# Hybrid decoder layer with 64 experts on one core: the experts' second weights requested by GpSimd on a second queue, the forget gate in column tiles, the last scatter in two halves

## The reference

```python
mod = (c_act @ ada_w[l] + ada_b[l]).reshape(B, N_MOD, D_MODEL)
h = rms_norm(x, mix_norm_g[l]) * (1.0 + scale_m) + shift_m
mix = mixer_sublayer(h, ...)           # pooling, spatial gating, convolution, attention with a forget gate
x = x + gate_m * mix
h = rms_norm(x, ffn_norm_g[l]) * (1.0 + scale_f) + shift_f
ffn = moe_ffn(h, ...)
x = x + gate_f * ffn
return rms_norm(x, final_norm_g)

# in the attention: four heads, a forget gate of four columns of w_in
log_f = jax.nn.log_sigmoid(f_logit.astype(jnp.float32))
cum = jnp.cumsum(log_f, axis=1)
logits = logits + c_blk[..., None] - cum_k[:, :, None, :]

# in the feed-forward part: 64 experts, 6 of them for each token, and one shared expert
a = jnp.einsum('td,edf->tef', tc, w1)
b = jnp.einsum('td,edf->tef', tc, w3)
hid = jax.nn.silu(a) * b * gc[:, :, None].astype(tc.dtype)
return jnp.einsum('tef,efd->td', hid, w2)
```

## Time and profile before

| | |
|---|---|
| time, median of 3 runs | 780.5 us (780.03 to 780.75) |
| profiled execution: time, span | 781.12 us, 779.3 us |
| mean granted TensorE clock | 0.989 |
| busy: PE, PEld, DVE, ACT, POOL | 730.0, 387.9, 326.3, 172.2, 8.7 us |
| moved by DMA | 271.33 MB, mean 348 GB/s |

### The profile page before, as it was taken

How to read it: one execution, slowest core, us unless ns; L and a number is a source line. 1 busy time by engine, 2 the same in 40 slices (tenths; PEclk the granted TensorE clock), 3 DMA queues, 4 the chain that set the end, 5 groups by cost and what they waited for, 6 DMA issues and landing times.

```text
span 779.3 us, 12407 instructions
## 1 busy us (share of the span) xinstructions
PE 730.0 (94%) x5000; PEld 387.9 (50%) x5000; DVE 326.3 (42%) x814; ACT 172.2 (22%) x344; POOL 8.7 (1%) x22
## 2 busy tenths in 40 slices
PE   4799999999999999999999999999999999899894
PEld 1388888888887444334333343333334333333232
DVE  1107675674446577333334233231333333323325
ACT  3213240200000241222222122121222222212213
POOL 0200001000000000000000000000000000000000
PEclk9799999999999999999999999999999999999998
DMA  9999535777869676999999999999999999999981
GB/s 339 378 349 365 190 108 189 237 260 259 264 221 385 262 274 240 392 422 421 421 417 420 419 420 421 421 421 408 409 420 422 420 419 422 421 421 420 421 353 55
DMA packets 73571, 271.33 MB, mean 348 GB/s; under 512 B 4440, under 2 KB 33248, under 8 KB 48688
## 3 DMA queue, kind: packets, MB, share of 16 engines
q1 hardware_dynamic: 71808, 264.26, 86.3%
q0 software_dynamic: 1408, 6.20, 2.1%
q10 hardware_dynamic: 304, 0.13, 0.1%
HBM read 269.51 MB, written 1.05 MB: 347 GB/s over the span
## 4 chain that ended last, share of the span: by engine, by line
PE 67%; DMA 21%; DVE 6%; SPq 3%; ACT 2%; issue 1%; DVEq 0%; ACTq 0%
PE bank L1118 65%; DMA ring<-exp_w_dram 19%; DMA ring<-ada_w_dram 2%; SPq L364 1%; DVE slot_gate L1054 1%; SPq L361 1%; PE bank L1438 1%; DVE reg L1058 1%; DVE reg L1049 1%; ACT reg L632 1%; DMA reg<-reg 1%; DVE h_hT L1109 0%; PE bank L1138 0%; DVE stats L1096 0%; DVE bank L1072 0%
## 5 line engine op out<-in xcount | busy, mean ns | idle before, releaser
L1118 PE MATMUL bank<-ring,h_hT 128*32 128x512 f32 (+2 forms) x2112 | 255.4, 586 | 14.3 <-DMA ring<-exp_w_dram 13.5
L1118 PEld LDWEIGHTS bank<-ring,h_hT 128*32 128x32 f32 (+1 forms) x2112 | 84.6, 113 | 170.8 <-issue 151.2
L1118 PE MATMUL bank<-h_hT,ring 128*128 128x256 f32 x704 | 158.4, 385 | 1.8 <-ACT h_hT L478 1.8
L1118 PEld LDWEIGHTS bank<-h_hT,ring 128*128 128x128 f32 x704 | 135.5, 193 | 21.4 <-ACT h_hT L478 2.0
L1118 PE MATMUL bank<-ring,const_misc 128*32 128x512 f32 x1008 | 116.5, 595 | 0.3
L1049 DVE TENSOR_TENSOR reg<-reg,bank 128x256 f32<-128x256 f32 x32 | 13.5, 421 | 180.7 <-ACT reg L632 180.7
L1072 DVE TENSOR_TENSOR bank<-bank,reg 128x512 f32<-128x512 f32 x64 | 44.5, 695 | 54.6 <-PE bank L1118 54.6
L1076 DVE TENSOR_TENSOR y_part<-bank,y_part 128x512 fp32r<-128x512 f32 x64 | 44.3, 692 | 42.4 <-ACT y_part L645 21.2
L1118 PEld LDWEIGHTS bank<-ring,const_misc 128*32 128x32 f32 x1008 | 30.2, 109 | 61.6 <-issue 57.3
L632 ACT ACTIVATE reg<-bank 128x256 f32<-128x256 f32 x32 | 12.3, 384 | 198.8 <-PE bank L1118 198.8
L1118 PE MATMUL bank<-take,h_part 128*128 128x256 f32 x288 | 50.6, 299 | 0.4 <-ACT h_hT L617 0.2
(11 more groups left out here) (231 smaller groups left out, 450.5 us busy)
## 6 DMA issues: line engine op xcount, KB each, us to landing
ring<-exp_w_dram SPq DMA_DIRECT2D x189, 1024.0 KB, 14.9
ring<-ada_w_dram SPq DMA_DIRECT2D x24, 1024.0 KB, 12.5
ring<-w_in_dram SPq DMA_DIRECT2D x24, 1024.0 KB, 12.3
ring<-w_branch_dram SPq DMA_DIRECT2D x4, 1024.0 KB, 12.9
ring<-w_out_dram SPq DMA_DIRECT2D x4, 1024.0 KB, 8.0
ring<-shared_w_dram SPq DMA_DIRECT2D x2, 1024.0 KB, 13.8
spare<-exp_w_dram SPq DMA_DIRECT2D x2, 1024.0 KB, 16.2
reg<-ada_bp_dram POOLq DMA_DIRECT2D x3, 512.0 KB, 8.3
```

The lines of the kernel that those rows point to most:

```text
L1118: return pe.matmul(o, lhsT, rhs, start=start, stop=stop, skip_group_check=True)
```

## The change

Three edits.

1. SP no longer requests second weights. GpSimd does, in a loop of its own that waits for `w2_used[r]` and goes by its own queue (the profile's q0, software; SP's is q1, hardware). For pairs 0 and 1 its requests stand before and after its request of `final_g`.
2. The forget gate's 8 matmuls write four groups of 32 partitions of bank 7 (the weights are padded from 4 to 32 columns), so that four can run side by side and the groups hold partial sums. ScalarE copies them (`f_tiles`), and one more matmul with a 0/1 matrix (`fold_f`) adds the groups, placed between the two halves of the key unit.
3. `y_split` becomes `y_low` and `y_high`: the gate matmul and the low half of a scatter wait for the low half alone, the high half of the scatter for the high one; the same after the last pair.

```diff
-MISC = {"wf": KD * HEADS, "sg_w": HEADS * P, ...}
+MISC = {"wf": KD * 32, "sg_w": HEADS * P, ...}
...
 @block.sync
-            def load_2(r, e, it):
-                sp.dma_start(ring[:, 6 * r + 4 + e, :],
-                             w2_src[bass.ds(it * (2 * RING_PAIRS) + (2 * r + e), 1)].rearrange("e p n -> (e p) n"))\
-                  .then_inc(w2_landed[r], 16)
...
             def load_step(use, it, spared=False):
                 for r in range(RING_PAIRS):
...
-                    sp.wait_ge(w2_used[r], use)
-                    for e in range(spared and r == SPARE_PAIR % 2, 2):
-                        load_2(r, e, it)
...
-                for e in range(2):
-                    sp.wait_ge(*used_up(LAST[6 * r + 4 + e]))
-                    load_2(r, e, 0)
...
 @block.gpsimd
+            def first_load_2(r):
+                for e in range(2):
+                    pool.wait_ge(*used_up(LAST[6 * r + 4 + e]))
+                    pool.dma_start(ring[:, 6 * r + 4 + e, :], w2_src[2 * r + e]).then_inc(w2_landed[r], 16)
+
+            first_load_2(0)
             pool.wait_ge(S["h2_done"], TB)
             pool.dma_start(final_g, a["final_norm_g"].rearrange("(o d) -> o d", o=1).partition_broadcast(P))\
                 .then_inc(S["final_in"], 16)
+            first_load_2(1)
+
+            def load_2(use, it, spared=False):
+
+                for r in range(RING_PAIRS):
+                    pool.wait_ge(w2_used[r], use)
+                    for e in range(spared and r == SPARE_PAIR % 2, 2):
+                        pool.dma_start(ring[:, 6 * r + 4 + e, :],
+                                       w2_src[bass.ds(it * (2 * RING_PAIRS) + (2 * r + e), 1)].rearrange("e p n -> (e p) n"))\
+                            .then_inc(w2_landed[r], 16)
...
 @block.scalar
             read_unit(2)
+            act.wait_ge(S["f_half"], 1)
+            act.activation(f_tiles[:, :], bank[7][:, 0:T], ACT.Copy).then_inc(S["f_tiled"], 1)
...
 @block.vector
-                           .then_inc(S["y_split"], 1)
+                           .then_inc(S["y_high" if hf else "y_low"], 1)
...
 @block.tensor
+            def forget_sum():
+                pe.wait_ge(S["f_tiled"], 1)
+                mm(bank[7][0:HEADS, T:2 * T], cn("fold_f"), f_tiles[:, :]).then_inc(S["f_done"], 1)
...
-                ins = mm(bank[7][0:HEADS, 0:T], wf[:, k, :], hT[:, k, :], k == 0, k == KD - 1)
-            ins.then_inc(S["f_done"], 1)
-            channels(3, ("mix", 3))
+                ins = mm(bank[7][32 * (k % 4):32 * (k % 4) + 32, 0:T], wf[:, k, :], hT[:, k, :], k < 4, k >= 4)
+            ins.then_inc(S["f_half"], 1)
+            channels(3, ("mix", 3), forget_sum)
...
-                        pe.wait_ge(S["y_split"], 2 * n)
+                        pe.wait_ge(S["y_low"], n)
...
                         scatter(1 - r, 0, opening)
+                        pe.wait_ge(S["y_high"], n)
                         scatter(1 - r, 1, opening)
...
-            last = passes * (2 * PAIRS)
-            pe.wait_ge(S["give_read"], passes * PAIRS)
-            pe.wait_ge(S["y_split"], last)
+            last = passes * PAIRS
+            pe.wait_ge(S["give_read"], last)
             for hf in range(2):
+                pe.wait_ge(S["y_high" if hf else "y_low"], last)
                 scatter(1, hf, stop=True).then_inc(S["sum_done"], 1)
```

More of the change, by code:

```diff
@@ L88 @@
 CONST = {"ident": 128, "upper": 128, "strict": 128, "ones": 256,
-         "fold": 64, "inv": 512, "iota": CAP, "thr": 3, "mask": 384}
+         "fold": 64, "fold_f": HEADS, "inv": 512, "iota": CAP, "thr": 3, "mask": 384}
 C_AT, C_W = {}, 0
@@ L101 @@
     P_W += _w
-MISC = {"wf": KD * HEADS, "sg_w": HEADS * P, "pool_w": 2 * P, "sg_g": BW, "sg_beta": BW, "sg_bias": 2 * T}
+MISC = {"wf": KD * 32, "sg_w": HEADS * P, "pool_w": 2 * P, "sg_g": BW, "sg_beta": BW, "sg_bias": 2 * T}
 M_AT, M_W = {}, 0
@@ L161, in mi @@
             return misc[:, M_AT[name]:M_AT[name] + MISC[name]].rearrange(pattern, **kw)
-        wf = mi("wf", "p (k h) -> p k h", h=HEADS)
+        wf = mi("wf", "p (k h) -> p k h", h=32)
         sgw = mi("sg_w", "p (h t) -> p h t", h=HEADS)
@@ L219, in decoder_layer @@
             logit = sig[:, 0:2, 0:384]
+            f_tiles = sig[:, 0, 0:T]
             v_sb = sig[:, 2, :].rearrange("p (b c) -> p b c", b=TB)
@@ L285, in decoder_layer @@
             final_in c_sig c_rep x_sq x_var x_rstd xn_done xT_done ada_done ada_read col_done acc_step ac_done h_done
-            unit_done f_done f_read exp_f cum_done cum_rows  conv_done
+            unit_done f_half f_tiled f_done f_read exp_f cum_done cum_rows  conv_done
             q_done k_done tv_done sigv_done v_var v_rstd vn_done tu_done sigu_done
@@ L294, in decoder_layer @@
             take_built pair_gates gate_mm slot_gated gathered gath_read first_read sig1_done th_done hid_done turn_done turn_read
-            sw2_gated x2_top give_read y0_done y_gated y_top y_split pos_next sum_done x3_sq x3_var x3_rstd fin_done stored""".split()
+            sw2_gated x2_top give_read y0_done y_gated y_top y_low y_high pos_next sum_done x3_sq x3_var x3_rstd fin_done stored""".split()
         S = {n: sem(n) for n in names}
@@ L452, in _ @@
                 .then_inc(S["final_in"], 16)
+            first_load_2(1)
[6 more added lines that the diff above has]
+                            .then_inc(w2_landed[r], 16)
+            with pool.Fori(1, SPARE_PAIR // 2) as it:
+                load_2(it, it)
+            load_2(SPARE_PAIR // 2, SPARE_PAIR // 2, True)
+            with pool.Fori(SPARE_PAIR // 2 + 1, STEPS - 1) as it:
+                load_2(it, it)
+            pool.wait_ge(S["npass_done"], 1)
+            passes = pool.value_load(n_pass[0:1, 0:1], min_val=1, max_val=MAX_PASS)
+            with pool.Fori(STEPS - 1, passes * STEPS) as use:
+                load_2(use, use % STEPS)
         @block.scalar
@@ L710, in _ @@
             dve.wait_ge(S["f_done"], 1)
-            dve.tensor_scalar(fz[:, 0, :], bank[7][0:HEADS, 0:T], par[0:HEADS, P_AT["b_f"]:P_AT["b_f"] + 1], None,
+            dve.tensor_scalar(fz[:, 0, :], bank[7][0:HEADS, T:2 * T], par[0:HEADS, P_AT["b_f"]:P_AT["b_f"] + 1], None,
                               ALU.add).then_inc(S["f_read"], 1)
@@ L1164, in begin_unit, with channels @@
                 return bank[B_UNIT[i % 2]], unit(u).rearrange("p (k n) -> p k n", k=KD)
-            def channels(i, u):
+            def forget_sum():
+                pe.wait_ge(S["f_tiled"], 1)
+                mm(bank[7][0:HEADS, T:2 * T], cn("fold_f"), f_tiles[:, :]).then_inc(S["f_done"], 1)
+            def channels(i, u, between=None):
                 b, w = begin_unit(i, u)
                 for m in range(2):
+                    if m and between:
+                        between()
                     for k in range(KD):
@@ L1501, in constants @@
     c["iota"][:] = np.arange(CAP)
+    c["fold_f"][:] = i % 32 == np.arange(HEADS)
     c["fold"][:] = i % E == np.arange(E)
@@ L1516, in lay_out @@
     par = np.concatenate(cols + [b_f], 1)
-    wf = inp["w_in"][0][:, COL["f"]:COL["f"] + HEADS].reshape(KD, P, HEADS).transpose(1, 0, 2).reshape(P, KD * HEADS)
+    wf = inp["w_in"][0][:, COL["f"]:COL["f"] + HEADS].reshape(KD, P, HEADS).transpose(1, 0, 2)
+    wf = np.pad(wf, ((0, 0), (0, 0), (0, 32 - HEADS))).reshape(P, KD * 32)
     sg_w = inp["sg_w"][0].transpose(2, 0, 1).reshape(P, HEADS * P)
```

## The result

The changed kernel takes 791.05 us (median of 4 runs, 790.34 to 791.75) against 780.62 us of before (4 runs), a ratio of 1.0131 with a 95% interval of 1.0117 to 1.0145: 10.3 us slower. The forecast was 786.1 us, in a range of 781 to 796. Direction and mechanism were right; the loss is nearly twice the sum. It also lies outside rival A's own range of 782 to 790 us: it fell into the stated range only because that range had room for rival B, a lower rate, which did not come. Two executions, one of before (1918 us) and one of `queue_alone` (4045 us), stand far off and are left out of every time and ratio in this document.

What follows compares the result with a forecast made beforehand. It took TensorE to bound the kernel from 99 to 270 us and the weight stream's order and rests late in the expert stage. +5.0 + 1.9 + 0.4 - 1.0 - 0.7 = +5.6 us gave 786.1 us, range 781 to 796.

Steps and rivals of the forecast that it cites:

- rival A: Whole kernel: the summed terms hold, half rate per queue and total rate unchanged; 782 to 790 us, chance 0.60.
- rival B: Expert stream: two queues at work move fewer bytes, 397 GB/s instead of 421; 794 to 802 us, chance 0.20.
- Turns: Expert weight stream: two queues with work alternate packet for packet, so with 8 KB rows each gets half the bytes.
- The order term: End of the expert stream: 2 MB more delivered ahead of pair 31's first weights, +5.0 us, bounds 0 and 5.0.
- The rest at pair 6: Early expert stage: transfer engines run out of requested work while pair 6 runs, +0.4 us, bounds 0 and 1.
- The rest at the shared expert: Between pairs 15 and 16: transfer engines rest 2.6 us instead of 0.7, net +1.9 us.
- The gate: Forget gate before the expert stage: side-by-side matmuls start the expert stage earlier, -1.0 us, bounds 0 and 2.3 gain.
- its wait for the small transfers: Before the logits: TensorE would wait about 1.4 us for two small transfers, against 0.37 us before.
- The scatter: Last scatter after pair 31: first half's matmuls run while VectorE makes the second half, -0.7 us, bounds -0.3 and -1.2.
- D: Expert stream: two queues at work move more bytes; 3% more rate gives 777 us, chance 0.06.
- C: Expert stream: requests served in order of asking, leaving only gate and scatter gains; 778.8 us, chance 0.08.

Runs made afterwards that it cites:

- queue_alone: The kernel before with only the second weights' requests moved to GpSimd, gate and scatter as before: 791.85 us, ratio 1.0152 to before.
- few_pairs: The changed kernel with GpSimd requesting second weights of pairs 8 to 15 and 28 to 31 only, SP the others: 788.16 us, ratio 1.0072 to before.
- act_queue: The changed kernel with the loop's second weights requested by ScalarE on its hardware queue, pairs 0 and 1 by SP: 790.3 us, ratio 1.0129 to before.
- second_half: The changed kernel with SP requesting second weights up to pair 15 and GpSimd for pairs 16 to 31: 782.47 us, ratio 1.0029 to before.
- first_half: The changed kernel with GpSimd requesting second weights of pairs 2 to 15 only, SP for 16 to 31: 787.21 us, ratio 1.0088 to before.

## Why the prediction was right, and where its sum was short

- **Turns.** "Half the bytes each" held in every kernel with two queues, and the order followed from it. Pair 31's first weights became the end of the stream.
- **The order term, +5.0 us.** It measured 4.9 us in the first stretch (`few_pairs`) and 4.8 in the second (4.1 to 5.9): 221.0 to 222.8 us, mean 221.7, in the change, `queue_alone`, `act_queue`, `second_half` and `few_pairs`, against 216.4 to 217.6, mean 216.9, in the five kernels with SP alone at the end.
- **The rest at pair 6, +0.4 us** (bounds 0 and 1), is 2.9 us. **The rest at the shared expert, +1.9 us**, is 4.8 against some 0.7 before, +4.1. These two terms are where the sum failed: 2.5 and 2.2 us too small. Both were worked out the same way, bytes still to come when a pair starts, less the time to the next packets, and both counts of bytes were too high. When pair 6 started, 3 MB were to come by the count, 3.15 million bytes; the queues of the change from then to the next request (387.88 to 394.95 us) show 1.25 and 1.05 million:

```profile
DMA packets 328, 2.32 MB, mean 328 GB/s; under 512 B 46, under 2 KB 46, under 8 KB 46
...
q1 hardware_dynamic: 183, 1.25, 42.6%
q0 software_dynamic: 144, 1.05, 35.9%
```

  GpSimd's 1 MB was still to come in full; of SP's 2 MB 0.8 million bytes had already been moved, 2.0 us. When pair 15 started, 12 MB or 12.58 million bytes were to come by the count, and the same view shows 11.82 million on the two queues (518.61 to 550.67 us), 1.8 us less. The other 0.4 to 0.5 us of each miss lie in the restart, for which the sum took 0.7 us. The reason for the bytes already moved: I had counted as if all 16 transfer engines stood where the landing stands, but a pair's weights have landed only when the last engine is done. At the end of the stream above, the shares from 760 to 765 us add up to 2.3 us, so that the average engine is done at 762.3 and the last near 764.8, 2.5 us apart. That this spread is what moved the bytes early is an argument: no row shows the engines apart, and no run takes the spread away. The prediction's own rows held a sign of it. For before, the same count gives 35 us of work against 32.6 us to the next packets, so no rest, yet the earlier trace rows show one. The prediction took the rest of before from the trace and that of the change from the count.
- **The accounting behind it.** The loss can be added up in two ways, which must not be mixed. By the stream, as the prediction did: one change of order at the end, and the longer rests, 5.0 + 2.9 + 4.1 us. By TensorE's stretches: a lag in each half, since in both kernels the transfer engines rest at the shared expert and the stream starts afresh behind it, and the rest at pair 6, 4.9 + 2.9 + 4.8 us. The 4.1 us of rest at the shared expert and the lag of the first half are one loss seen twice. With the rests at their measured size the prediction's way gives 780.6 + 7.0 - 2.4 = 785.2 us for `first_half`, inside its interval (784.8 to 790.1) like the 786.0 of the other. So its accounting was sound, and only the sizes of the rests were not.
- **The gate, -1.0 us, is -1.7.** The request of the two small transfers came 9.9 us behind the gate's start instead of 10.8, near the 1.1 us of the sum. They also landed faster; the timelines of ScalarE and of TensorE in the change:

```profile
65.32 1.21 ACTq L526 DMA_DIRECT2D reg<-reg  x1
```

```profile
71.66 2.86 PE L1136 MATMUL bank<-reg 66*128 66x128 f32 x16 [0.42 <-DMA reg<-reg]
```

  6.3 us from the request to the logits, where before it was 7.2; the eleven kernels with the gate edit have 6.3 to 6.5, the three without it 7.2. Why, no run was made to tell. TensorE itself saved 1.8 us up to the end of the key unit (8.7 us behind the gate's start instead of 10.6), not 2.3, so its wait for the small transfers was 0.42 us, not the 1.4 forecast. That the gain of 1.7 us is inside its bounds owes half to the faster landing, which the prediction had not foreseen.
- **The scatter, -0.7 us**, is -0.7.
- **Rivals B and D** (another rate with two queues) are out with 8 KB rows: 420 to 422 GB/s. **C** (order does no harm) is out.

The terms as measured, by the stretches: +7.8 in the first and +4.8 in the second for the queue, -1.7 and -0.7 for the others, +10.2 us. By the stream they are 5.0 + 2.9 + 4.1 - 1.7 - 0.7 = +9.6 us. The times give +10.3, with an interval of 9.1 to 11.3 that holds both.

## What to carry to other kernels

Where a stream of transfers sets the pace, one queue in the order of need is a schedule; a second queue brought no more bandwidth here (421 GB/s with one and with two) but laid a claim on every other packet, and what is asked for on it goes ahead of what the compute engine waits for. Put there only what is needed before the head of the first queue, or what finds the engines idle. When you estimate how long the transfer engines still have work at the moment of a landing, take off what they have already moved of the next transfers (about 2 us of work here). Try the count on the kernel before as well: where it misses a rest that the trace shows, it will miss more of it after. And look for the places where the ring runs dry: a lag is paid again behind each of them.

## What the runs showed of the hardware

Two queues with work share the transfer engines packet for packet: 760 to 761 packets with 2 to 1 in bytes. It is the same for GpSimd's software queue and for ScalarE's hardware queue. With 8 KB rows the sum stays at 421 GB/s, with 4 KB rows on one of them it is 416. After waits of 4.30 and 7.59 us TensorE ran at a granted clock of 0.50, so that the 32 matmuls with first weights of `few_pairs`' pair 28 took 8.89 us instead of 7.07. When a pair's first weights had landed, the transfer engines had already moved some 0.8 million bytes of the next ones, 2 us of work. And the same code before the forget gate took up to 3.3 us more or less from one profile to the next, more than the gate edit and the scatter edit are worth together (2.4 us).
